# One core, two transformer blocks in fp32: first block's attention in batches of a query tile, index scores and top-k rounds among the projections

## What is computed

```python
h = jnp.einsum('bsd,dc->bsc', x, w_in[l])
a_q, a_k, a_v, b_q, b_k, b_v, i_q, i_k, i_w, c_q, c_kv, c_kr = split_cols(h)
o_a = sliding_window_sink_attn(...)    # 8 heads, window 128, a sink per head
o_b = indexer_sparse_attn(...)         # 4 heads, over the 128 keys with the best index score
o_c = mla_attn(...)                    # 4 heads of 64 + 32 dims, causal
mix = jnp.concatenate([o_a, o_b, o_c], axis=-1)
x = layer_norm(DEEPNORM_ALPHA * x + jnp.einsum('bsm,md->bsd', mix, w_out[l]), ...)
x = layer_norm(DEEPNORM_ALPHA * x + moe_ffn(x, ...), ...)
```

## Time and profile before

| what | us |
|---|---|
| median of 3 runs (3807.23 to 8128.77) | 3812.29 |
| profiled execution | 3800.46 |
| its span, first to last instruction | 3798.7 |
| mean granted TensorE clock | 0.898 |

### The profile page before, as it was taken

The page is one execution under the profiler, slowest core; times in us unless marked ns, Lnnn a source line. Parts: engine busy times, 40 slices in busy tenths (PEclk is TensorE's granted clock), DMA queues, the critical chain, the costliest instruction groups (busy, mean ns, idle before and its releaser), DMA issues.

```text
span 3798.7 us, 42690 instructions
## 1 busy us (share of the span) xinstructions
PE 3430.3 (90%) x14478; PEld 2641.8 (70%) x14478; DVE 2028.5 (53%) x3448; ACT 1448.2 (38%) x2224; POOL 290.2 (8%) x203
## 2 busy tenths in 40 slices
PE   8889788888987988799997899989999889879998
PEld 6546666666556766578875688867887667658886
DVE  4783576646855676554537553546343543455343
ACT  4543466635433566422222322233222444432221
POOL 0001022210001122200000100010000000010000
PEclk9767799989567999899998899989999889889998
DMA  3101199712001699222321222323223211012232
GB/s 120 37 1 42 37 307 314 265 40 69 1 1 58 219 318 303 77 86 94 94 94 36 67 97 94 99 73 127 94 94 120 96 39 62 28 34 94 96 99 76
DMA packets 174977, 389.48 MB, mean 103 GB/s; under 512 B 11313, under 2 KB 70065, under 8 KB 174193
## 3 DMA queue, kind: packets, MB, share of 16 engines
q1 hardware_dynamic: 173424, 377.45, 30.2%
q0 software_dynamic: 1408, 10.23, 0.8%
HBM read 381.34 MB, written 6.29 MB: 102 GB/s over the span
## 4 chain that ended last, share of the span: by engine, by line
PE 70%; DVE 13%; DMA 7%; ACT 4%; DVEq 3%; issue 2%; SPq 0%; POOL 0%; ACTq 0%; POOLq 0%
PE ps L507 18%; PE ps L509 18%; PE ps L508 17%; DMA gate_up_stage<-in_w_gu 7%; PE ps L584 4%; PE ps L600 4%; DVE moe_lo L1478 4%; PE ps L590 2%; ACT moe_hi L903 2%; PE ps L655 1%; PE ps L724 1%; PE ps L557 1%; DVE tmp L1688 1%; DVE xs_lo L1676 1%; PE ps L574 1%
## 5 line engine op out<-in xcount | busy, mean ns | idle before, releaser
L1224 DVE TENSOR_TENSOR w_lo<-w_stage,w_hi 128x1024 fp32r<-128x1024 f32 (+3 forms) x360 | 461.8, 1283 | 956.0 <-ACT w_hi L903 953.1
L507 PE MATMUL ps<-xs_hi,w_hi 128*128 128x512 f32 (+1 forms) x2032 | 825.0, 406 | 109.8 <-DVE xs_lo L1676 75.2
L509 PE MATMUL ps<-xs_hi,w_lo 128*128 128x512 f32 (+1 forms) x2032 | 813.4, 400 | 0.0
L508 PE MATMUL ps<-xs_lo,w_hi 128*128 128x512 f32 (+1 forms) x2032 | 813.1, 400 | 0.0
L903 ACT ACTIVATE w_hi<-w_stage 128x1024 fp32r<-128x1024 f32 (+3 forms) x360 | 393.3, 1092 | 1038.1 <-PE ps L509 1024.5
L507 PEld LDWEIGHTS ps<-xs_hi,w_hi 128*128 128x128 f32 (+1 forms) x2032 | 389.2, 192 | 227.7 <-issue 74.3
L509 PEld LDWEIGHTS ps<-xs_hi,w_lo 128*128 128x128 f32 (+1 forms) x2032 | 390.1, 192 | 90.6
L508 PEld LDWEIGHTS ps<-xs_lo,w_hi 128*128 128x128 f32 (+1 forms) x2032 | 391.4, 193 | 85.3
L1478 DVE TENSOR_TENSOR moe_lo<-gate_up_stage,moe_hi 128x1024 fp32r<-128x1024 f32 x224 | 277.9, 1281 | 137.4 <-ACT moe_hi L903 137.1
L507 PE MATMUL ps<-h_hi,w_hi 128*128 128x512 f32 x704 | 276.8, 393 | 0.0
L509 PE MATMUL ps<-h_hi,w_lo 128*128 128x512 f32 x704 | 276.5, 393 | 0.0
(11 more groups left out here) (322 smaller groups left out, 4925.5 us busy)
## 6 DMA issues: line engine op xcount, KB each, us to landing
gate_up_stage<-in_w_gu SPq DMA_DIRECT2D x112, 1024.0 KB, 6.1
w_stage<-in_f_gu SPq DMA_DIRECT2D x174, 512.0 KB, 3.5
down_stage<-in_w_dn SPq DMA_DIRECT2D x112, 512.0 KB, 5.4
w_stage<-in_f_dn SPq DMA_DIRECT2D x64, 704.0 KB, 4.1
w_stage<-in_w_in SPq DMA_DIRECT2D x28, 512.0 KB, 3.4
w_stage<-in_d_qk SPq DMA_DIRECT2D x24, 512.0 KB, 3.5
w_stage<-in_w_out SPq DMA_DIRECT2D x16, 512.0 KB, 3.5
w_stage<-in_d_v SPq DMA_DIRECT2D x12, 512.0 KB, 3.5
```

The lines of the kernel that those rows point to most:

```text
L507: pe.matmul(o, lh, rh, start=start, stop=False)
L508: pe.matmul(o, lh, rl_, start=False, stop=False)
L509: return pe.matmul(o, ll, rh, start=False, stop=stop)
L1224: tt(w_lo[:, s, 0:n], stage[:, s, 0:n], w_hi[:, s, 0:n].bitcast(F32), ALU.subtract).then_inc(w_split, 1)
```

## The change

- Attention runs in 12 **batches**, one per kind and query tile: A (8 units each, query tile by query tile), C, B (4 units each). The probabilities are not normalised before the mix. The mix has `prob_t` as weights (128 columns) and moves 64 columns of v; queries are partitions of its result. A batch's results lie in one PSUM bank. DVE adds the sinks, takes one reciprocal per batch and multiplies the whole batch (`normalise`); TensorE turns it back (`turn_rows`), ACT takes the high part, DVE the low part, once per batch.
- The sink's exp is one ACT operation per batch of A.
- The projections run as straight code in another order (`FIRST`): index heads first, then v of B, c, k_rope, v of A, the rest. Two index scores follow each of jobs 5 to 10, with their relu and sums. 23 rounds of top-k follow in DVE's steps 6 to 16 (`ROUNDS_EARLY`), the other 25 in attention.
- The norm of c stands in DVE's step 11, its spread after job 12, its use in steps 13 and 14.
- The first output job reads tiles 6, 7 ahead of 4, 5, and waits for the last batches only there.
- In the second block's attention (`attend_wide`) the code is written apart, with waits on renumbered counts.

```diff
+FIRST = [("head", 8), ("head", 9), ("head", 10), ("vb", 0), ("c", 0), ("c", 1), ("c", 2), ("kr", 0), ("va", 0), ("head", 4),
+         ("head", 0), ("head", 1), ("head", 2), ("head", 3), ("head", 5), ("head", 6), ("head", 7), ("up", 0)]
+F_SIZE = {"head": W_FULL, "c": W_FULL, "va": W_FULL, "vb": W_VB, "kr": W_KR, "up": W_UP}
+ROUNDS_EARLY = {6: 2, 7: 2, 8: 3, 9: 2, 10: 2, 11: 2, 12: 2, 13: 2, 14: 2, 15: 2, 16: 2}
+BATCHES = 12
...
-        def units():
-
-            for t in range(4):
-                for h in range(2):
-                    for qt in range(NT):
-                        r, k0 = slice(64 * h, 64 * h + 64), max(qt - 1, 0)
-                        yield dict(q=heads[r, t, qt * P:qt * P + P], keys=[(heads[r, 4, k0 * P:qt * P + P], 0)],
...
+        def batches():
+
+            for qt in range(NT):
+                k0 = max(qt - 1, 0)
+                yield dict(sinks=True, tiles=slice(0, 4), at=qt * P, units=[
+                    dict(q=heads[64 * h:64 * h + 64, t, qt * P:qt * P + P],
+                         keys=[(heads[64 * h:64 * h + 64, 4, k0 * P:qt * P + P], 0)],
+                         W=(qt - k0 + 1) * P, mask=mask_a[:, (0 if qt else P):2 * P], scale=0.125,
+                         sink=4 * h + t, col=4 * h + t, o=P * t + 64 * h,
+                         v=[va[:, b, 64 * h:64 * h + 64] for b in range(k0, qt + 1)]) for t in range(4) for h in range(2)])
+            for qt in range(NT):
+                yield dict(sinks=False, tiles=slice(6, 8), at=qt * P, units=[
...
-        UN, UD = list(units()), [list(units_d(e)) for e in range(2)]
+        BA, UD = list(batches()), [list(units_d(e)) for e in range(2)]
+        UN = [dict(un, B=B, last=i == len(ba["units"]) - 1) for B, ba in enumerate(BA) for i, un in enumerate(ba["units"])]
+        LAST = [n for n, un in enumerate(UN) if un["last"]]
...
-        DEEP = dict(ring=4, scores=3, exps=2, mix=1, o_hi=2, o_lo=3, banks=(2, 3, 0, 1))
-        WIDE = dict(ring=3, scores=2, exps=1, mix=0, o_hi=1, o_lo=1, banks=(2, 4))
+        S_BANKS, S_RING = (2, 3, 1), 4
...
+                for i, k in enumerate(order or range(K)):
...
-                                 hi[:, k, :], lo[:, k, :], k == 0, k == K - 1)
+                                 hi[:, k, :], lo[:, k, :], i == 0, i == K - 1)
...
+            def attend(l):
+
+                c0, N = l * UNITS, len(UN)
+
+                def mix(n):
+                    un = UN[n]
+                    ba, nb = BA[un["B"]], un["W"] // P
+                    if un is UN[0] or UN[n - 1]["last"]:
+                        if un["B"] >= 2:
+                            pe.wait_ge(rows_ready, l * BATCHES + un["B"] - 1)
+                    pe.wait_ge(pt_copied, c0 + n + 1)
+                    for i in range(nb):
+                        last = pe.matmul(ps[:, 6 + un["B"] % 2, un["o"]:un["o"] + 64], probt[:, n % 2, i * P:i * P + P], un["v"][i],
+                                         start=i == 0, stop=i == nb - 1)
+                    last.then_inc(o_full, 1)
+
+                def turn_rows(B):
+                    nt = BA[B]["tiles"].stop - BA[B]["tiles"].start
+                    pe.wait_ge(rows_ready, l * BATCHES + B + 1)
+                    if B > 0:
+                        pe.wait_ge(ot_split, l * BATCHES + B)
+                    for i in range(nt):
+                        last = pe.transpose(ps[:, 0, i * P:i * P + P], rows_o[:, B % 2, i * P:i * P + P], ident[:, :])
+                    last.then_inc(ot_full, 1)
+
+                for n in range(3):
+                    scores(UN[n], n, S_BANKS)
+                for n in range(N + 5):
+                    if n < N:
+                        pe.wait_ge(p_exp, c0 + n + 1)
+                        transposes(UN[n], n, prob, 4 + n % 2, S_RING)
+                    if n + 3 < N:
+                        pe.wait_ge(masked, c0 + n + 1)
+                        scores(UN[n + 3], n + 3, S_BANKS)
+                    if 0 <= n - 1 < N:
+                        mix(n - 1)
+                    if n - 4 in LAST:
+                        turn_rows(LAST.index(n - 4))
...
-                for i in range(4):
...
+                for i in range(17):
+                    job(j + i // 2, i % 2, c + i // 2, i % 2, xs_hi, xs_lo, M={"kr": 64, "vb": 68}.get(FIRST[i][0], P),
                         waits=(xs_ready, l * 16) if i == 0 else None)
-                job(j + 2, 0, c + 2, 0, xs_hi, xs_lo)
-                job(j + 2, 1, c + 2, 1, xs_hi, xs_lo, M=68)
-                pe.wait_ge(const_landed, 144)
-                turn(2 * l, 0, P, 5)
-                turn(2 * l + 1, 1, 68, 6)
-                stats(l, [sum2, sum1])
-                with pe.Fori(0, 5) as i:
-                    for s in range(2):
-                        job(j + 3 + i, s, c + 3 + i, s, xs_hi, xs_lo)
-                spread(3 * l, [RB, MB])
-                job(j + 8, 0, c + 8, 0, xs_hi, xs_lo)
+                    if i == 4:
...
+                            pe.wait_ge(const_landed, 144)
+                        turn(2 * l, 1, 68, 6)
+                    if i == 9:
+                        turn(2 * l + 1, 0, P, 5)
+                        stats(l, [sum2, sum1])
+                    if i == 12:
+                        spread(3 * l, [RB, MB])
+                    for n in range(12):
+                        if 5 + n // 2 == i:
+                            index_scores(n)
...
+                attend(l)
+
+                def mixed(k):
+                    if k == 0:
+                        pe.wait_ge(ot_split, l * BATCHES + 8)
+                    if k == 4:
+                        hold(pe, ot_split, l * BATCHES + BATCHES)
+
+                with_stats(l * 16, lambda m: job(j + 9 + m // 2, m % 2, c + 12 + (m + 1) // 2, 1 - m % 2, xs_hi, xs_lo,
+                                                 before=mixed if m == 0 else None,
+                                                 order=(0, 1, 2, 3, 6, 7, 4, 5) if m == 0 else None), x)
...
+            def attend(l):
...
+                def exps(n):
+                    un = UN[n]
+                    B, i, b = un["B"], un["col"], n % S_RING
+                    act.wait_ge(masked, c0 + n + 1)
+                    if n == 0 or UN[n - 1]["last"]:
+                        if B >= 2:
+                            act.wait_ge(rows_ready, l * BATCHES + B - 1)
+                    nc.scalar.activation(prob[:, b, 0:un["W"]], prob[:, b, 0:un["W"]], ACT.Exp, bias=nmax[:, B % 2, i:i + 1],
+                                         scale=-1.0, accum_out=sums_a[:, B % 2, i:i + 1]).then_inc(p_exp, 1)
+                    if un["last"] and BA[B]["sinks"]:
+                        act.wait_ge(sink_in, l * NT + B + 1)
+                        nc.scalar.activation(sink_e[:, B % 2, :], sink_e[:, B % 2, :], ACT.Exp).then_inc(sink_done, 1)
...
+                    if n - 5 in LAST:
+                        B = LAST.index(n - 5)
+                        ba = BA[B]
+                        act.wait_ge(ot_full, l * BATCHES + B + 1)
+                        nt = ba["tiles"].stop - ba["tiles"].start
+                        copy(xs_hi[:, ba["tiles"], ba["at"]:ba["at"] + P],
...
+                for i in range(17):
+                    kind, n = FIRST[i]
+                    if i + 2 < 18:
+                        split(j + (i + 2) // 2, i % 2, F_SIZE[FIRST[i + 2][0]], 2 * c + i + 1)
+                    else:
+                        split(j + 9, 0, W_FULL, 2 * c + 17)
+                    if kind == "head":
+                        rotate(2 * c + i, i % 2, True)
...
+                    for n in range(12):
+                        if 5 + n // 2 == i:
+                            index_relu(n)
+                    if i == 13:
+                        for n in range(3):
+                            act.wait_ge(c_tile, 3 * l + n + 1)
+                            copy(cs_hi[:, n, :], cfeat[:, n, :]).then_inc(c_hi_done, 1)
...
+            def top_round(work):
+
+                v.drain()
+                V.max(max8[:, :], work)
+                v.drain()
+                V.match_replace(work, max8[:, :], work, TAKEN)
...
+            def attend(l, rounds):
...
+                def normalise(B):
...
+                    v.wait_ge(p_exp, c0 + LAST[B] + 1)
...
+                        v.wait_ge(sink_done, l * NT + B + 1)
+                        tt(total, total, sink_e[:, s_, :], ALU.add)
+                        v.drain()
+                    V.reciprocal(rinv[:, s_, 0:nh], total)
+                    v.drain()
+                    v.wait_ge(o_full, c0 + LAST[B] + 1)
+                    if B >= 2:
+                        v.wait_ge(ot_full, l * BATCHES + B - 1)
...
+                    tt(o, src, r, ALU.mult).then_inc(rows_ready, 1)
...
+                def low(B):
...
+                    v.wait_ge(ot_hi_done, l * BATCHES + B + 1)
+                    tt(xs_lo[:, at[0], at[1]], ps[:, 0, 0:nt * P].rearrange("p (a n) -> p a n", n=P),
```

(47 more changed lines are left out.)

## The result

| | before | after |
|---|---|---|
| median of the runs | 3809.8 us (4 runs) | 3702.9 us (4 runs) |
| ratio to before | | 0.9725, interval 0.9704 to 0.9746 |
| span of the profiled execution | 3798.7 us | 3697.1 us |

One of the four runs before took 8128.8 us, in a slower state; the ratio compares the three others, 3805.1 to 3812.3 us, with the four after.

A forecast was written before the change was run, and what follows sets the result against it. TensorE, busy 90% of the span, was taken as the bound. Per layer, attention +8.3 and projections -0.4 gave +7.9, twice +16 us: 3816 for the profiled execution, 3828 on the median; range 3755 to 3865.

The forecast's parts named there:

- The clock of C, and the waits behind the rounds: Attention, C: clock left as before, mean 0.74; C forecast at 51.2 us, from 52.7 before.
- one stand of 4.4 us: End of C: TensorE stands while DVE does two rounds and final masks; moving rounds out removes 4.4 us per layer.
- The clock of B: Attention, B: TensorE-bound at clock 0.50 (1.2 GHz), and costed at that clock after the change too.
- A at 1.2 GHz: Attention, A: TensorE-bound at the low clock; a unit of 256 columns stays at 2.8 us.
- rival (d): Attention: full clock throughout, about 107 us against 187, giving 3668 us; chance 0.05.
- +0.05 a unit for the mix's first load: Attention mix: uncovered first load grows from 64 to 128 columns, 0.05 us for each of 64, +3.2 us per layer.
- rival (c): Attention mix: costs half with 64 moving columns, 29 us less per layer, giving 3770 us; chance 0.08.
- The forecast of -0.4 us: Projections per layer: index stage removed -14.3, DVE backlog +13.6, a turn among earlier jobs +0.3.
- the queue that I followed: Projections after job 5: DVE's work and waits total 91.7 us before q_c, 78.1 before; TensorE stands 4.3 at the spread.
- (b): Projections: DVE doesn't fall behind, so the +13.6 us per layer goes, giving 3801 us; chance 0.20.
- (e): Projections: TensorE keeps 1.2 GHz through jobs 6 to 16, 53 us more per layer, giving 3933 us; chance 0.05.
- case (a): Attention, C: stays at 1.2 GHz, 5.2 us more per layer, giving 3838 us; chance 0.26.

The follow-up runs named there:

- the last run: Changed kernel with zeros beside A's and B's keys (scores on 128 rows) and the 25 attention rounds spread up to unit 42: 3642.1 us, ratio 0.9571.

## Why the prediction was wrong

**The clock of C, and the waits behind the rounds: the step that failed.** I wrote "I leave its clock as it was, since its scores and transposes are the same and its records come as densely". The profile of before held the answer in the rows between those of the earlier trace rows. Two lines of its timeline of TensorE, in C, two windows of 1 us there (the clock during these waits and after them), and what TensorE waited for from C's first mix to B's (us in total, times, longest):

```profile
251.31 0.44 PE L590 MATMUL ps<-ident,prob 128*128 128x128 f32 x2 [0.66 <-DVE prob L1337]
252.26 0.40 PE L600 MATMUL ps<-prob_t,v_c 128*64 128x128 f32 x2 [0.51 <-ACT prob_t L903]
...
252.00:253.00 1.00, 0.74 (x4) 0.49 (x4) 0.91 (x5) 0.80 (x4) 0.00 (x0) 1.00 0.00 0
255.00:256.00 1.00, 1.00 (x4) 0.58 (x3) 0.92 (x3) 0.76 (x3) 0.00 (x0) 0.50 0.00 0
...
PE ps L590 <- DVE prob L1337: 8.1, 7, 4.7
PE ps L600 <- DVE xs_lo L1316: 2.3, 5, 0.6
PE ps L600 <- ACT prob_t L903: 1.0, 2, 0.5
```

By its windows the clock rose four times between 232 and 274 us, and fell each time during or after such waits, the last time within the stand ahead of B (4.7 us on TensorE, where I had 4.4 from DVE's rows). I had read the mean of 0.74 as a property of the stretch. I had also written that DVE "is then last" in C, and yet counted the rounds' removal as one stand of 4.4 us: TensorE's waits there were 11.4 us in all, and the clock that was lost with them came on top. Against the forecast C came out 25.9 us a layer shorter. Keeping all rounds in attention brings C back to 44.1 us and B to 47.8; moving them early with the old attention gives 31.2 and 27.3.

**The clock of B.** "B is TensorE-bound at 0.50" was true and I took it as B's own level. It was what B had been handed: the stand at the end of C lay just ahead of it, and the clock fell within it. Entered at 2.4 GHz B takes 26.2 us after the change, entered at 1.2 GHz 47.8 to 49.8 in the runs above. Against the forecast it is 22.7 us a layer.

**A at 1.2 GHz** was right, but I had no reason for it. The runs give one: with scores on 64 rows the clock was held where it was full and TensorE had no wait, and rose in no run; with 96 or 128 rows it rose. So rival (d), full clock through attention, was half right: C and B, not A. I gave it 0.05 and wrote "For it only the last units, without scores, and parts of C": just the units in which no 64-row scores stand.

**The gaps of a unit.** I put +0.05 a unit for the mix's first load. In its place 0.19 went away. One unit of A after, at 0.50 (its mix, transposes and scores, then the next mix), and one with C's 96-row scores in it:

```profile
184.58 1.11 PE L618 MATMUL ps<-v_a,prob_t 128*128 128x64 f32 x4
185.49 0.63 PE L602 MATMUL ps<-ident,prob 128*128 128x128 f32 x2
186.05 1.22 PE L596 MATMUL ps<-heads 64*128 64x256 f32 x2
187.20 1.11 PE L618 MATMUL ps<-v_a,prob_t 128*128 128x64 f32 x4
...
224.73 0.95 PE L618 MATMUL ps<-v_a,prob_t 128*128 128x64 f32 x4
225.47 0.63 PE L602 MATMUL ps<-ident,prob 128*128 128x128 f32 x2
225.90 0.63 PE L596 MATMUL ps<-k_c,q_c 96*128 96x128 f32 x2
226.33 0.95 PE L618 MATMUL ps<-v_a,prob_t 128*128 128x64 f32 x4
```

From start to start the mix takes 0.91 us (1.04 by my terms before: four records and 0.19), the transposes 0.56 (0.62), the scores 1.15 as before: 2.62 for 2.81. Eight units of one block at 1.55 (their starts 155.6 and 157.2) and 24 at 2.62 make 75.3; four turns at 0.85 (I had 1.04) add 3.4; three units with C's scores save 1.02 each, 0.59 of it gaps and 0.43 a second block of scores. That is 75.6, measured 75.5. The term of the loads in A was +1.6 and is -6.1, 7.7 of the 11.7 us by which A was off; the turns were 0.8 shorter than forecast. The other 3 are at its border: before, scores of 128, 256 and 384 columns stood between the last units, now three of 128, and TensorE waited for DVE there for 0.73, 0.88 and 0.62 us (at 237.3, 239.2 and 240.3). How these share the 3 us was not measured.

**The mix at half, rival (c),** did not come: the records stay 0.21 us apart at 0.50. That "the weight load sets the pace" fits this. With the half-width mixes, the fp32 shapes of attention fit one price: a record costs as much as the larger of its weight columns and its moving columns. Before it was 64 and 128, after 128 and 64, the same price. The rule that I had weighed there, the Trainium skill, TensorE: Matmul & The Clock Gate, section Back-to-back issue gap, has a formula for a single matmul that goes by the moving columns alone. By it this mix would take half of the one before; the trace has the same 0.21 us a record, and so sides with the same section's warning that a stream is set by loads and matmuls both.

**Projections.** The forecast of -0.4 us was nearly right as a sum: -1.9 us to the first transposes in layer 0; in layer 1, from the first output job of layer 0 to the first transposes, +0.8 (614.2 for 613.4). The stand of 4.1 and the q_c 90.7 us after job 5 bear out the queue that I followed, and refute (b), no backlog, and (e), a clock lost for all the jobs: from 46 to 96 us it is 1.00, and from 101 to 121. The rounds' share of the backlog of 12.6 us is 6.0, by the run that has none of them early; what the rest of it consists of no run takes apart.

**Range and chances.** The prediction said that every term but clock and backlog was under 4 us a layer; the gaps of A were off by 7.7, and C and B, most of it the clock, by 48.6. The range let the clock of C go down, case (a), and gave the way up 0.05. With evidence in the same stretch of rows for both, that was too narrow.

## What stays open

The runs change the rows of the scores and with them the gap around the group, so they can't say which of the two the clock answers to. The old mix and the half-width one, which keep a gap of 0.20 in every unit, did not prevent a rise. Which waits cost the full clock is open too: 1.73 us in C did not in the last run, while in the order C, A, B it was gone 0.4 us into a wait. Why what follows layer 1's first output job became 3.8 us longer (2669.5 us, 2665.7 before) has no explanation here.

## What to carry to other kernels

Read the granted clock as a state with a history, not as a property of a stretch: find what the engine did before each fall and each rise, and ask of every removed wait what stands behind it at which clock. What in these runs could only hold the full clock, the units with 64-row scores, belongs directly behind work that raises it, with no wait on another engine in between, and an engine's filler work belongs where the clock is low anyway. Where half of the rows of a matmul lie idle, try zeros in them: here that took 59.2 us instead of 75.5 for A.

## What was not expected of the hardware

- Units with scores on 64 rows neither raised the clock in 48 us of uninterrupted work (B in the order A, B, C) nor lost it in 42 us (A without rounds, 1.00). 96 rows, and 128, raised it.
- A stop of 2.14 us at 2.4 GHz cost B 21.6 us; behind waits of 1.18 and 0.44 us A and B lost theirs. With 96-row scores a wait of 1.73 us left it at 1.00.
- A group of 64-row scores between full-width groups costs 0.29 us of its own at 1.2 GHz, and 0.17 and 0.13 on the mix and the transposes around it; with 96 rows all three are gone (a unit of 2.19 us by its parts takes 1.60). The Trainium skill, TensorEngine Tiling (Array Packing), section Key Properties, says that a change of tiling mode drains the engine; these gaps fit that, and the 96-row scores, which have none, behave as a full array.
- The fp32 records of attention cost as much as the larger of their weight and moving columns: 0.21 us at 1.2 GHz for 64 by 128 and for 128 by 64, 0.105 for 64 by 64.
